# Boundaries by token groups, reordered splits and sums, and eight modulation units moved beside feed-forward products, in a two-block transformer kernel on one core

## The reference, cut to what matters

```python
def _modulation(cond, w, b):                       # w: 1024 x 9216
    m = jax.nn.silu(cond) @ w + b
    return jnp.split(m[..., None, :], N_MOD, axis=-1)   # N_MOD = 9

def _prenorm(h, gain, shift, scale):
    return _rmsnorm(h, gain) * (1.0 + scale) + shift

for layer in range(DEPTH):                         # DEPTH = 2
    last = layer == DEPTH - 1
    sh1, sc1, g1, shm, scm, gm, sh2, sc2, g2 = _modulation(c, ada_w[layer], ada_b[layer])
    csh1, ...                                 = _modulation(c_ctx, ada_w[layer], ada_b[layer])
    h  = h  + 0.5 * g1 * _swiglu(_prenorm(h, norm_ffn1[layer], sh1, sc1), ffn1_w_in[layer], ffn1_w_out[layer])
    hc = hc + 0.5 * cg1 * _swiglu(_prenorm(hc, norm_ffn1[layer], csh1, csc1), ...)
    ...                                            # the mixer: layer 0 "even", layer 1 "odd"
    h = h + gm * (mix_l @ mix_w_out[layer])
    h = h + 0.5 * g2 * _swiglu(_prenorm(h, norm_ffn2[layer], sh2, sc2), ffn2_w_in[layer], ffn2_w_out[layer])
    ...                                            # hc the same, but not in the last layer
return _rmsnorm(h, final_norm)                     # then a second network of two layers on 256 tokens
```

## Time and profile before

| | us |
|---|---|
| median of 3 runs | 2960.15 |
| lowest and highest | 2960.11, 2967.92 |
| the profiled execution, its own time | 2971.95 |
| its span, first to last instruction | 2970.1 |
| TensorE busy in the span | 2911.5 (98%) |
| VectorE busy | 1932.5 (65%) |
| ScalarE busy | 1316.3 (44%) |
| mean granted clock of TensorE | 0.992 |

### The profile page before, as it was taken

How to read it: one execution, slowest core, us unless ns; L and a number is a source line. 1 busy time by engine, 2 the same in 40 slices (tenths; PEclk the granted TensorE clock), 3 DMA queues, 4 the chain that set the end, 5 groups by cost and what they waited for, 6 DMA issues and landing times.

```text
span 2970.1 us, 51963 instructions
## 1 busy us (share of the span) xinstructions
PE 2911.5 (98%) x20058; PEld 2597.0 (87%) x20058; DVE 1932.5 (65%) x3070; ACT 1316.3 (44%) x1964; POOL 0.2 (0%) x4
## 2 busy tenths in 40 slices
PE   9999999999999999999999999999999999999999
PEld 6888888878888888888888999999899999998998
DVE  5856763646747666334666667677776776777666
ACT  4332333423222332223345655555655555556555
POOL 0000000000000000000000000000000000000000
PEclk9999999999999999999999999999999999999999
DMA  8645642054546545332423666455456645554564
GB/s 247 198 119 177 188 131 78 30 156 146 169 125 184 169 138 154 102 98 77 128 86 92 180 177 179 134 164 170 142 150 198 177 143 150 165 165 143 161 191 138
DMA packets 614443, 439.45 MB, mean 148 GB/s; under 512 B 22172, under 2 KB 578040, under 8 KB 614136
## 3 DMA queue, kind: packets, MB, share of 16 engines
q1 hardware_dynamic: 613268, 436.70, 49.7%
q10 hardware_dynamic: 996, 0.23, 0.0%
HBM read 430.84 MB, written 1.05 MB: 145 GB/s over the span
## 4 chain that ended last, share of the span: by engine, by line
PE 89%; DVE 7%; ACT 1%; issue 1%; SPq 1%; DMA 1%; DVEq 0%; ACTq 0%
PE ps L489 27%; PE ps L490 26%; PE ps L491 26%; DVE wlo L438 2%; DMA raw<-ffn_w_in 1%; PE ps L580 1%; PE ps L2005 1%; ACT whi L431 1%; PE ps L2017 1%; SPq L760 1%; PE ps L1985 1%; PE ps L908 1%; PE ps L1013 0%; PE ps L1463 0%; PE ps L1214 0%
## 5 line engine op out<-in xcount | busy, mean ns | idle before, releaser
L489 PE MATMUL ps<-xh,whi 128*128 128x256 f32 (+1 forms) x3856 | 1230.4, 319 | 24.4 <-DVE wlo L438 10.2
L490 PE MATMUL ps<-xl,whi 128*128 128x256 f32 (+1 forms) x3856 | 1208.5, 313 | 0.0
L491 PE MATMUL ps<-xh,wlo 128*128 128x256 f32 (+1 forms) x3856 | 1208.5, 313 | 0.0
L438 DVE TENSOR_TENSOR wlo<-raw,whi 128x1024 fp32r<-128x1024 f32 x732 | 868.2, 1220 | 169.5 <-ACT whi L431 166.9
L431 ACT ACTIVATE whi<-raw 128x1024 fp32r<-128x1024 f32 x731 | 747.8, 1053 | 431.7 <-PE ps L491 364.4
L489 PEld LDWEIGHTS ps<-xh,whi 128*128 128x128 f32 x3856 | 732.8, 190 | 101.4 <-issue 44.9
L491 PEld LDWEIGHTS ps<-xh,wlo 128*128 128x128 f32 x3856 | 730.8, 190 | 46.5
L490 PEld LDWEIGHTS ps<-xl,whi 128*128 128x128 f32 x3856 | 731.6, 190 | 44.4
L489 PE MATMUL ps<-hid_h,whi 128*128 128x256 f32 (+1 forms) x1116 | 364.7, 327 | 0.0
L491 PE MATMUL ps<-hid_h,wlo 128*128 128x256 f32 (+1 forms) x1116 | 362.8, 325 | 0.0
L490 PE MATMUL ps<-hid_l,whi 128*128 128x256 f32 (+1 forms) x1116 | 362.7, 325 | 0.0
(11 more groups left out here) (406 smaller groups left out, 2620.8 us busy)
## 6 DMA issues: line engine op xcount, KB each, us to landing
raw<-ffn_w_in SPq DMA_DIRECT2D x176, 512.0 KB, 5.4
mod_pair<-ada_w SPq DMA_DIRECT2D x48, 1024.0 KB, 5.3
raw<-w_in SPq DMA_DIRECT2D x96, 512.0 KB, 4.5
raw<-w_ffn_in SPq DMA_DIRECT2D x88, 512.0 KB, 4.7
raw<-w_gate SPq DMA_DIRECT2D x64, 512.0 KB, 4.0
mod_w<-ada_w SPq DMA_DIRECT2D x24, 1024.0 KB, 10.0
raw<-ffn_w_out SPq DMA_DIRECT2D x64, 384.0 KB, 3.7
raw<-ffn_w_out SPq DMA_DIRECT2D x64, 320.0 KB, 3.7
```

Of the source, the lines that this page charges most:

```text
L438: nc.vector.tensor_tensor(split_at(unit, wlo, s, h), raw[:, s, h, :], split_at(unit, whi, s, h).bitcast(F32), ALU.subtract).then_inc(S("lo ...
L489: nc.tensor.matmul(dst, w_h, x_h, start=start, stop=False)
L490: nc.tensor.matmul(dst, w_h, x_l, start=False, stop=False)
L491: return nc.tensor.matmul(dst, w_l, x_h, start=False, stop=stop)
```

## The change

Five edits. (1) Units of the modulation: at the norm "ffn2" 4 units are done in place of 8, at the norm "ffn1" none in place of 4; the 8 go beside feed-forward products. Feed-forward 2 of layer 0 still has twice five pairs (other units than before), feed-forward 1 of layer 1 has five pairs in its first half (before four) and three in its second (before none). (2) The two units on each side of a halved boundary (`half_units`) get the skew of 16 elements: the last two of the stage before and the first two behind it, at "ffn2" one before and two behind, at "odd" two and three. (3) So that writers and readers know each unit's number, the three pairs ahead of such a boundary's end are written out (`unroll`), and the even mixer passes `c.units + u`. (4) At the boundary "ffn2" the splits of the next unit 0 move from the output stage into the norm, behind the last squares, as at the other boundaries. (5) In every norm but "odd" both halves of unit 1 are split ahead of the second root and reciprocal (before: one ahead, one behind), and VectorE's copy of the modulation rows comes behind them and not ahead.

```diff
-MOD_BESIDE = {("ffn1", 0): ((0, 8, 5), (0, 18, 5)), ("ffn2", 0): ((1, 4, 5), (1, 14, 5)), ("ffn1", 1): ((1, 28, 4), None)}
-MOD_AT_NORM = {"mix": (0, 28, 4, 3, 4), "ffn2": (0, 32, 8, 5, 6), "ffn1": (1, 24, 4, 3, 4)}
+MOD_BESIDE = {("ffn1", 0): ((0, 8, 5), (0, 18, 5)), ("ffn2", 0): ((1, 0, 5), (1, 10, 5)), ("ffn1", 1): ((1, 20, 5), (1, 30, 3))}
+MOD_AT_NORM = {"mix": (0, 28, 4, 3, 4), "ffn2": (0, 32, 4, 3, 4)}
-ROWS_FIRST = {"mix": 3, "ffn2": 5, "ffn1": 3}
+ROWS_FIRST = {"mix": 3, "ffn2": 3}
...
-        token_units = set()
+        token_units, half_units = set(), set()
         def split_at(u, w, s, h):
-            first = TOKEN_SKEW if u in token_units else SKEW if u >= SKEW_FROM else 0
+            first = TOKEN_SKEW if u in token_units else SKEW if u >= SKEW_FROM or u in half_units else 0
...
                 elif stage == "norm":
+                    if args[7] in HALVED:
+                        half_units.update({"odd": range(c.units - 2, c.units + 3), "ffn2": range(c.units - 1, c.units + 2)}
+                                          .get(args[7], range(c.units - 2, c.units + 2)))
...
-                    pairs_of(pe, c, 4 - by_tail, down, first=True, before=rest)
+                    pairs_of(pe, c, 4 - by_tail, down, first=True, before=rest, unroll=by_tail)
...
-                        w_h, w_l = half_of(c.units, s, h, DC // 2, 256)
+                        w_h, w_l = half_of(c.units + u, s, h, DC // 2, 256)
...
# ScalarE, norm_by_halves
-                if name != "ffn2":
-                    act_split(act, 0, 0, c.units, (0,))
+                act_split(act, 0, 0, c.units, (0,))
                 root_of_half(0)
-                if name != "ffn2":
-                    act_split(act, 0, 0, c.units, (1,))
+                act_split(act, 0, 0, c.units, (1,))
...
-                act_split(act, 0, 1, c.units + 1, (0,))
+                act_split(act, 0, 1, c.units + 1)
                 second_root()
-                act_split(act, 0, 1, c.units + 1, (1,))
                 highs(1, 0, DC)
...
# ScalarE, output stage
-                    act_split(act, 0, 0, c.units + 2)
                     done = c.units + 2 + CREDIT
...
# VectorE, norm_by_halves
+                dve_split(dve, 0, 0, c.units, (0,))
                 if name != "ffn2":
-                    dve_split(dve, 0, 0, c.units, (0,))
                     add(0, 1)
                 reciprocal(0)
-                if name != "ffn2":
-                    dve_split(dve, 0, 0, c.units, (1,))
+                dve_split(dve, 0, 0, c.units, (1,))
                 pieces(0, {2: add_second, 4: lambda: squares(1, 1)})
+                if name == "odd":
+                    return lambda: reciprocal(1), lambda: pieces(1)
+                dve_split(dve, 0, 1, c.units + 1)
+                reciprocal(1)
                 if at_norm:
                     norm_mods_copy(at_norm)
-                if name == "odd":
-                    return lambda: reciprocal(1), lambda: pieces(1)
-                dve_split(dve, 0, 1, c.units + 1, (0,))
-                reciprocal(1)
-                dve_split(dve, 0, 1, c.units + 1, (1,))
                 pieces(1)
...
# VectorE, output stage
-                        dve_split(dve, 0, 0, c.units + 2, (0,))
-                        add(0, 0)
                         for b in range(2):
                             sq_add(4 + b, b, args[1])
-                        dve_split(dve, 0, 0, c.units + 2, (1,))
+                        add(0, 0)
                         add(1, 0)
                         squares(0, 0)
                         squares(1, 0)
```

More of the change, by code:

```diff
@@ L593, in build @@
             [MOD_AT_NORM[name][2] for name in ("mix", "ffn2")] + beside_units(("ffn2", 0)) + \
-            [MOD_AT_NORM["ffn1"][2]] + beside_units(("ffn1", 1))
+            beside_units(("ffn1", 1))
         assert sum(mod_groups) == 2 * MOD_UNITS
         norm_tiles = {"ffn2": [w[:, :, :] for w in mod_w0]}
-        norm_tiles["mix"] = norm_tiles["ffn1"] = [mod_w[:, 0], mod_w[:, 1], mod_w2[:, :, :], mod_w3[:, :, :]]
-        norm_landed = {"mix": 0, "ffn2": 1, "ffn1": 2}
+        norm_tiles["mix"] = [mod_w[:, 0], mod_w[:, 1], mod_w2[:, :, :], mod_w3[:, :, :]]
+        norm_landed = {"mix": 0, "ffn2": 1}
         def mod_group(layer, m0):
@@ L662, in build @@
                 ("gains", layer, 0, "norm_ffn1"),
-                ("norm", hT, 2, sh(0), g(0), False, PAIR, "ffn1", "ffn1"),
+                ("norm", hT, 2, sh(0), g(0), False, PAIR, None, "ffn1"),
             ]
@@ L676, in build @@
                 ("ffn", io["ffn2_w_in"][layer], io["ffn2_w_out"][layer], nc_ * T, (layer, 2), False,
-                 MOD_BESIDE.get(("ffn2", layer), none), False, 0 if layer else PAIR, None if layer else "ffn1",
+                 MOD_BESIDE.get(("ffn2", layer), none), False, 0 if layer else PAIR, None,
                  None if layer else "ffn1"),
@@ L1359, in tok_unit @@
                         for k in range(DC):
-                            w_h, w_l = half_of(c.units, s, 2 * k // DC, DC // 2, 256)
+                            w_h, w_l = half_of(c.units + u, s, 2 * k // DC, DC // 2, 256)
                             j = k % (DC // 2)
@@ L2363, in ffn @@
                     if n == 1 and tail in HALVED:
-                        pairs_of(act, c, 3, square_former, ahead=act_split, first=True)
+                        pairs_of(act, c, 3, square_former, ahead=act_split, first=True, unroll=True)
                         act_split(act, 0, 1, c.units + 1)
@@ L3188, in ffn @@
                     if n == 1 and tail in HALVED:
-                        pairs_of(dve, c, 3, down, ahead=dve_split, first=True)
+                        pairs_of(dve, c, 3, down, ahead=dve_split, first=True, unroll=True)
                         dve_split(dve, 0, 1, c.units + 1)
```

## The result

| | runs | median, us | lowest to highest |
|---|---|---|---|
| before | 4 | 2962.33 | 2960.11 to 2967.92 |
| after | 4 | 2942.64 | 2941.97 to 2944.92 |

The ratio is 0.9932, with a 95% interval of 0.9915 to 0.9949: 20 us faster, where 26.85 against 2960.15 were forecast. The time lies 9.3 us above the forecast and 0.6 above the end of its range. Before alone had 2960.15 as the median of three runs, 2962.33 with the fourth.

The account below looks back on a forecast made before the run. TensorE, busy 2911.5 of 2970.1 us, bounds the kernel; only its waits, slow stretches and movable work pay. Terms 16.65 ("ffn2") + 3.3 ("mix") + 2.2 ("ffn1") + 4.7 (skew) = 26.85; 2960.15 - 26.85 = 2933.3 us, range 2925 to 2942.

Parts of the forecast that it names:

- Waits at "ffn2": TensorE's wait for the last sum of squares saves 5.9 us, its split wait 2.65; a new stall for pieces costs 0.7.
- Half rate: Matmuls at half clock behind the waits return to full rate: 2.5 and 2.7 us at "ffn2", 1.5 "mix", 1.3 "ffn1".
- Rows (3.6) and added pairs (-3.3): Four units of modulation rows fewer at "ffn2" save 3.6 us; four pairs more in feed-forward 1 of layer 1 cost 3.3.
- R4: Rival, chance 0.02: VectorE doesn't keep up in the second half of feed-forward 1 of layer 1; 2981 us without cover.
- "mix" (3.3): At boundary "mix" the wait of 1.77 us for the split and 1.5 of half rate go, 3.3 in sum.
- "ffn1" (5.5 before the pairs): At boundary "ffn1" 4.2 us of rows and wait and 1.3 of half rate go; net 2.2 after the added pairs.
- Written-out pairs: Two more written-out pairs at three boundaries: at worst 2.4 us slower, taken as 0.
- Skew: 1176 half-wide boundary matmuls start 2.4 to 7 ns sooner with the skew, 4.5 taken: 4.7 us saved, ends 2.8 to 8.2.
- R1: Rival, chance 0.15: the skew of the boundaries' half-wide units gives nothing; 2938.0 us.
- R2: Rival, chance 0.14: the clock falls all the same at the boundaries, each fall costing 1.3 to 2.7 us; 2936.6 with two.
- R3: Rival, chance 0.06: the first wait at "ffn2" is the chain of sums, not the load, and partly stays; 2939 us.
- From the sum to the time: Whole kernel: the profiled execution lies 11.80 us above the median, so 26.85 comes off the median 2960.15, giving 2933.3.

Follow-up runs that it names:

- the order with the skew: Changed kernel with the tables of units of before, so no unit moved: 2944.50 us, ratio 0.9929 to before.
- the units left at "ffn1": Changed kernel, but the four modulation units of "ffn1" stay at that norm and two pairs are added, not four: 2941.94 us, ratio 0.9919 to before.
- the order alone: Kernel before with only the order of splits, sums and the copy changed on ScalarE and VectorE: 2943.84 us, ratio 0.9926.
- the moved units: Kernel before with only the tables of modulation units changed as in the change: 2954.22 us, ratio 0.9955.

## Why the prediction was wrong in its number

*Waits at "ffn2" (5.9, 2.65, less 0.7).* Right: 5.88 and 2.96 went, and a new stall came of about 0.5, spread over the distances between matmuls of unit 0. Either edit removes the first wait, and the sum did not say so.

*Half rate (2.5 and 2.7 at "ffn2", 1.5 at "mix", 1.3 at "ffn1").* Right in the trace: from the sum's start to the rows 6.15 became 3.78, and from unit 1's start to its full pace 5.96 became 3.29. But a clock fall is not bound to a wait as the steps had it: the one at "mix" came in the mixer once. The terms were worked out on the first profile, with a mean clock of 0.992. Over the 34 runs of before on two of the chips it was 0.9933 and 0.9938, over both sets of the changed kernel 0.9965 and 0.9970.

*Rows (3.6) and added pairs (-3.3).* Right: 1.7 + 1.8, and -3.6. Each of the four pairs cost 0.9, not 0.8, and VectorE did not become the bound (R4): TensorE has no wait in the half stage of 111.06.

*"mix" (3.3) and "ffn1" (5.5 before the pairs).* Right: without the skew 46.87 to 43.53 is 3.3, and 47.85 to 41.97 is 5.9. The waits for pieces were smaller than taken, 0.9 in all, the one for the split 0.86. The 7.5 that the step gives for rows and wait doesn't follow from the earlier trace rows: four units of rows (3.7) and 2.96 are 6.7; the sum doesn't use it.

*Written-out pairs (0).* Right: the stretch to "ffn1" holds two of them more and took 332.80 and 332.79.

*Skew (4.7).* Failed: 2.24, below its lower bound of 2.8. The step took the earlier trace rows as two samples of one pace and went between 117.6 and 113.3. They were two states, between which no long run lies, and the boundaries are nearly all in the slower one; the one longer exception, some hundred matmuls in "ffn1" of the second profile, is what makes 40.88 of 41.3. (The bounds of 2.4 and 7 ns fit a pace of 120.0 without the skew, not the 120.8 named beside them.) R1, no effect, is excluded by the paces all the same. Place alone moved the half-wide pace from 120 to 117.8 and the full-wide one from 227 to 233. The prediction read a rule of the Trainium skill ("SBUF — State Buffer", section "SBUF: two separate sides": TensorE never waits on anyone) as saying that the place would not matter. That reading fails; the rule itself speaks of other users of the memory, and whether TensorE met one there no run shows. R2 and R3 did not come: no fall in a boundary of the four profiles, no rest of the first wait.

*From the sum to the time.* This is the step that failed: "the profiled execution lies 11.80 above the median, so the forecast is 2960.15 - 26.85". It takes the excess for a constant of both kernels. In the first comparison it was 9.6 for before and 2.3 for after. Part was the anchor: three runs gave 2960.15, 2962.33 with a fourth, and later sets 2965.6 or more. Of the 9.3 us missed in the first comparison 2.2 are that, 2.4 what the landmarks gave less than the sum (24.5 against 26.85; the skew alone 2.5), and 4.8 what is in the traces' difference and not in the medians' (24.5 against 19.7). Where these 4.8 are was not shown, and chance is not excluded: for two kernels near the changed one, the order with the skew and the units left at "ffn1", the medians gave 25.3 and 24.7 where the landmarks gave 23.9 and 25.0. Two things point to before's profiles: the mean clock of before is 0.9933 to 0.9938 over all its runs and 0.9928 over its four profiles, worth 1.5 to 3 us, and a long stage that can run 5.7 us faster never did so in four profiles of before. What a run without a trace did in that stage can't be seen. The interval of the ratio, 0.9915 to 0.9949, is itself 10 us wide.

## What to carry to other kernels

A sum against one profiled execution forecasts another profiled execution; to reach a median, carry the ratio or difference to a median of many runs, and widen the range by the scatter of both kernels (here some 10 us each). When two edits remove one wait, price each with the other already made: the order alone gave nearly all of this change, and the moved units, which look like the larger edit, about 1 us on top of it (11.4 without it). When one matmul shape shows two paces, ask whether they are two states rather than two samples, before taking a value between.

## What the hardware showed

- Half-wide matmuls of one shape, at full clock, with no wait: 119.7 to 120 ns with weights at offset 0, 118.3 at 32 bytes, 113.3 or 117.8 at 64, 118.7 at 96 and 128, 117.8 at 192. Full-wide ones: 227.0 at 0, 233.3 at 64 and 232.5 at 128. Which of the two paces at 64 bytes a stage takes can change from one execution to the next and then holds for hundreds of matmuls. What sets it was not found.
- The times of kernels with 64 bytes in layer 1 scatter by 10 us and more where many runs were made (before: 2960 to 2975 over 25 runs on one chip). With 32 bytes and one pace, ten runs lay within 3.4 us. That the paces make the scatter is suggested by this, not shown: with 192 bytes and one pace in the profile, ten runs spread over 9.4.
- A wait of 1.77 us was followed by half clock in three of the four profiles of before, and in one not until some 48 us later. Waits of 0.9 and less were not followed by it in the boundaries of either kernel. It also came without any: in the changed kernel's first profile at 1824.0 and 2400.9, and in the second profile of before at 468.6, TensorE had no idle time over 0.3 us in the 25 us ahead. The first of these is a place that recurs: in seven of the eight profiles of the two kernels a fall lies 428 to 436 us behind the start of "odd".
